# The gates of the last 128 tokens: scattered into DRAM by adding transfers instead of built by matmuls

## The reference, cut to what matters

```
idx  = i1[ci // 16] * 128 + i2[ci % 16]                 # 16 experts of each head and token
gate = softmax(sc)                                      # over the 16
act  = gelu(einsum('thed,td->the', u_table[idx], x))    # u, v: 16384 x 1024
y    = einsum('the,thed->td', gate * act, v_table[idx])
```

## Time and profile before

| | |
|---|---|
| median of 3 runs | 1456.25 us (1448.58 to 1458.06) |
| profiled execution | 1457.33 us, its span 1455.5 us |
| granted TensorE clock, mean | 0.995 |
| busy: PE, DVE, POOL, ACT | 98%, 82%, 53%, 44% |
| moved by DMA | 423.15 MB, 291 GB/s over the span |

### The profile page before, as it was taken

How to read it: one execution, slowest core, us unless ns; L and a number is a source line. 1 busy time by engine, 2 the same in 40 slices (tenths; PEclk the granted TensorE clock), 3 DMA queues, 4 the chain that set the end, 5 groups by cost and what they waited for, 6 DMA issues and landing times.

```text
span 1455.5 us, 24698 instructions
## 1 busy us (share of the span) xinstructions
PE 1427.1 (98%) x8813; PEld 1367.2 (94%) x8813; DVE 1187.4 (82%) x2337; ACT 637.1 (44%) x1035; POOL 768.0 (53%) x428
## 2 busy tenths in 40 slices
PE   7999889999999999999999999899999999999998
PEld 6879678888999999999999999899999999999998
DVE  5747463388989999989999897678899998998994
ACT  4463472222433333447777775332343333433332
POOL 2524171233577678865555555256566665566630
PEclk9999999999999999999999999999999999999999
DMA  7400211322579989999999999989999999999991
GB/s 271 152 30 1 116 30 47 106 69 72 165 249 351 319 311 346 411 391 333 365 363 350 363 395 393 396 304 410 410 410 410 410 409 410 411 410 410 410 360 58
DMA packets 165902, 423.15 MB, mean 291 GB/s; under 512 B 13348, under 2 KB 85924, under 8 KB 163912
## 3 DMA queue, kind: packets, MB, share of 16 engines
q1 hardware_dynamic: 119624, 254.48, 46.9%
q0 software_dynamic: 46208, 167.81, 30.2%
HBM read 376.00 MB, written 46.20 MB: 290 GB/s over the span
## 4 chain that ended last, share of the span: by engine, by line
PE 91%; DMA 4%; DVE 2%; issue 1%; ACT 1%; DVEq 0%; SPq 0%; ACTq 0%
PE banks L2052 33%; PE banks L1816 16%; PE banks L2123 10%; PE banks L2125 10%; PE banks L2124 10%; PE banks L2091 5%; DMA act_in<-act_scratch 3%; PE banks L2031 1%; PE banks L1846 1%; DMA u_raw<-in_uT 1%; PE banks L1890 1%; PE banks L1948 1%; PE banks L1968 1%; PE banks L1967 1%; DVE x_res L1635 1%
## 5 line engine op out<-in xcount | busy, mean ns | idle before, releaser
L822 POOL DMA_INDIRECT rows<-in_v,idx x160 | 286.1, 1788 | 189.2 <-DVE x_res L1635 129.0
L2123 PE MATMUL banks<-w_hi,v_hi 128*128 128x352 f32 x1024 | 330.0, 322 | 1.8 <-DVE w_lo L1734 1.7
L2124 PE MATMUL banks<-w_lo,v_hi 128*128 128x352 f32 x1024 | 329.3, 322 | 0.0
L2125 PE MATMUL banks<-w_hi,v_lo 128*128 128x352 f32 x1024 | 329.3, 322 | 0.0
L1161 ACT ACTIVATE v_hi<-v_raw 128x1024 fp32r<-128x1024 f32 x128 | 134.5, 1059 | 287.3 <-DMA v_raw<-in_v 287.0
L822 POOL DMA_INDIRECT rows<-in_u,idx x160 | 191.1, 1195 | 122.0 <-DVE z L1617 85.5
L798 POOL TENSOR_TENSOR u_lo<-u_raw,u_hi 128x1024 fp32r<-128x1024 f32 x66 | 164.0, 2488 | 95.4 <-ACT u_hi L1056 52.7
L2052 PE MATMUL banks<-h_lo,u_hi 128*128 128x352 f32 x1024 | 198.0, 328 | 0.0
L2123 PEld LDWEIGHTS banks<-w_hi,v_hi 128*128 128x128 f32 x1024 | 192.3, 188 | 2.8 <-issue 2.6
L2052 PE MATMUL banks<-h_hi,u_hi 128*128 128x352 f32 x1024 | 191.2, 328 | 3.7 <-ACT act_kept L1082 3.7
L2124 PEld LDWEIGHTS banks<-w_lo,v_hi 128*128 128x128 f32 x1024 | 192.3, 188 | 0.0
(11 more groups left out here) (284 smaller groups left out, 2084.7 us busy)
## 6 DMA issues: line engine op xcount, KB each, us to landing
u_raw<-in_uT SPq DMA_DIRECT2D x128, 512.0 KB, 6.7
v_raw<-in_v SPq DMA_DIRECT2D x128, 512.0 KB, 15.5
gate_scratch<-stage SPq DMA_DIRECT2D x11, 2048.0 KB, 12.1
gate_pairs<-gate_scratch SPq DMA_DIRECT2D x15, 1408.0 KB, 18.3
act_scratch<-act_out SPq DMA_DIRECT2D x116, 176.0 KB, 7.0
act_in<-act_scratch SPq DMA_DIRECT2D x29, 704.0 KB, 16.0
wi_raw<-in_w_in SPq DMA_DIRECT2D x8, 1024.0 KB, 7.2
wq_raw<-in_w_q SPq DMA_DIRECT2D x8, 1024.0 KB, 5.6
```

The costliest lines, as they stand in the source:

```text
L822: nc.gpsimd.indirect_dma_start(ROW_KB[U_SLOT[s]][:], None, a["u"] if kind in "ab" else v_flat, bass.IndirectOffsetOnAxis(ap=at_x, axis=0)) ...
L2123: mm(y, v_hi[x][:, ds], w_hi[q][:, j, :], start=start, stop=False)
L2124: mm(y, v_hi[x][:, ds], w_lo[q][:, j, :], start=False, stop=False)
L2125: return mm(y, v_lo[x][:, ds], w_hi[q][:, j, :], start=False, stop=stop)
```

## The change

- The dense tokens 384 to 511 get no gate matrices. `BUILT` chunks (7 of 11) are built: 224 tokens, 56 batches. Blocks before the gates are 88 (`PRE`), the blocks with gates 88 to 119.
- Their part of the gates' DRAM tensor is cleared by 16 transfers of 512 KB on SP's queue in the first part, from a tile of zeros.
- GpSimd scatters their gates: for each of the 128 slots one indirect transfer with addition, 128 elements of 4 bytes from column `x` of `tri` to cells whose numbers are in `idx3`. Three or four scatters follow each block from 66 to 112, 16 in five blocks and none in the sixth; before the first of a head GpSimd waits until all scatters of the head before have landed, since two heads may add to one cell.
- `choose(3)` computes the cell numbers in floats on VectorE instead of row and column tiles.
- Low parts of u: up to block 63 GpSimd makes three of four (before: one of two), then one of four.
- Dots: 1.25 for each block up to 61, then about 1.7.

```
-PRE_BODY, PRE_TRIPS = 4, 18
-MAIN_BODY, MAIN_TRIPS = 8, 6
+BUILT = CHUNKS - P // CHUNK
+BATCHES = BUILT * CHUNK // BATCH
+PRE_BODY, PRE_TRIPS = 4, 22
+MAIN_BODY, MAIN_TRIPS = 8, 4
...
+SHARED = [n for n in range(SHARE_FROM, POST) if (n % 4 != 3 if n < TRI_TRIP * PRE_BODY else n % 4 == 0)]
+SCATTER = {66 + 6 * h + j: (h, (0, 4, 7, 10, 13, 16)[j:j + 2]) for h in range(PH) for j in range(5)}
+DOTS = [""] * POST + ["aa"] * 3 + ["a"] + [""] * 4
+for _n in range(SHARE_FROM - 2, POST):
+    DOTS[_n] = "a" * (1 + (_n % 4 == 3 if _n < NORM_AT else _n % 2 or _n % 8 == 2 or _n % 16 == 6))
+for _n in range(NORM_AT, PRE + 2 * MAIN_BODY):
+    if "".join(DOTS).count("b") < NE:
+        DOTS[_n] = DOTS[_n][:-1] + "b"
...
+            def clear(m):
+                sp.dma_start(gate_d[m, :, BUILT:].rearrange("p c n t -> p (c n t)").rearrange("p (x e) -> p x e", e=P),
+                             zeros[:].unsqueeze(1).to_broadcast([P, (CHUNKS - BUILT) * PAIR * CHUNK // P, P])).then_inc(gates_cleared, 16)
+            sp.wait_ge(zeros_ready, 1)
             for r in range(3, UNITS):
                 load_unit(r)
+                for m in range(2):
+                    clear(2 * (r - 3) + m)
...
+            def scatter(h, k0, k1):
+                if h == k0 == 0:
+                    pool.wait_ge(idx3_ready, 1)
+                    pool.wait_ge(tri_ready, 2 * (TB - 2) + 1)
+                    pool.wait_ge(gates_cleared, 16 * NK // PAIR)
+                if k0 == 0 and h:
+                    pool.wait_ge(gates_scattered, 16 * TOPK * h)
+                for x in range(h * TOPK + k0, h * TOPK + k1):
+                    nc.gpsimd.indirect_dma_start(
+                        gate_cells, bass.IndirectOffsetOnAxis(ap=idx3[:, x:x + 1], axis=0),
+                        tri[:, TB - 2, 0, x:x + 1], None, compute_op=ALU.add).then_inc(gates_scattered, 16)
...
                     pool.wait_ge(share_open, SHARED.index(n + 2) + 1)
                     split_u(n + 2)
+                if n in SCATTER:
+                    h, (k0, k1) = SCATTER[n]
+                    scatter(h, k0, k1)
...
+            sp.wait_ge(gates_scattered, 16 * SLOTS)
             sp.dma_start(gates[:].rearrange("p c n t -> p c (n t)"), half_pair(SAVED // PAIR, 1)).then_inc(gates_in, 16)
```

More of the change, by code:

```diff
@@ L66 @@
 V_ATT, V_ML, V_CQ, V_CKV, V_BI, V_BF = 0, 8, 12, 14, 15, 16
-V_W = 17
+V_AT = 17
+V_W = 18
 E_BLOCKS = NK
@@ L100 @@
 assert MAIN_BATCHES * MAIN_TRIPS >= BATCHES > MAIN_BATCHES * (MAIN_TRIPS - 1) and MAIN_BATCHES * BATCH == 2 * CHUNK
-EXP_TRIP, TRI_TRIP = PRE_TRIPS - 3, PRE_TRIPS - 2
+EXP_TRIP, TRI_TRIP = 15, 16
 NORM_AT, TAB_AT = 62, 68
[L105 to L113, removed]
+SHARED = [n for n in range(SHARE_FROM, POST) if (n % 4 != 3 if n < TRI_TRIP * PRE_BODY else n % 4 == 0)]
[6 more added lines that the diff above has]
+        DOTS[_n] = DOTS[_n][:-1] + "b"
 U_DOTS = SLOTS + NE
@@ L119 @@
 assert ALL_DOTS.count("b") == NE
-assert ALL_DOTS.count("a") == SLOTS
+assert ALL_DOTS.count("a") == SLOTS, ALL_DOTS.count("a")
 ALL_DOTS += "w" * (NE - ALL_DOTS.count("w")) + "v" * SLOTS
@@ L129 @@
 DOTS_PRE = dots_before(PRE)
-GELU_TRIP = 4
+GELU_TRIP = 2
 ADDS_LEFT = GATHERS - dots_before(E_BLOCKS)
@@ L335, in build @@
         acc_b = at("acc_b", 182, [P, D])
+        zeros = at("zeros", 207.25, [P, P])
+        idx3 = at("idx3", 204, [P, SLOTS], I32)
         idx0 = at("idx0", 20, [P, SLOTS], I32)
@@ L436, in build @@
         tri_ready = sem("tri_ready")
+        zeros_ready = sem("zeros_ready")
+        gates_cleared = sem("gates_cleared")
+        gates_scattered = sem("gates_scattered")
+        idx3_ready = sem("idx3_ready")
         triT_done = sem("triT_done")
@@ L500, in lo_slot, with low_parts, wait_ulo @@
             return n % 4 if n < POST else n % 2
-        def wait_ulo(eng, i, base, body):
+        def low_parts(n):
+            at_pool = min(n + 1, POOL_FIRST) + sum(m <= n for m in SHARED)
+            return (ulo_pool, at_pool) if n < POOL_FIRST or n in SHARED else (ulo_dve, n + 1 - at_pool)
+        def wait_ulo(eng, i, base, body, trip=1):
             if isinstance(i, int):
[L505 to L517, removed]
+                eng.wait_ge(*low_parts(i * body + base))
+                return
+            made, at_trip = low_parts(trip * body + base)
+            each = low_parts((trip + 1) * body + base)[1] - at_trip
+            eng.wait_ge(made, i * each + (at_trip - trip * each))
         def staged_at(b):
@@ L553, in _ @@
             sp.dma_start(pos_i[:], a["positions"]).then_inc(pos_in, 16)
+            def clear(m):
+                sp.dma_start(gate_d[m, :, BUILT:].rearrange("p c n t -> p (c n t)").rearrange("p (x e) -> p x e", e=P),
+                             zeros[:].unsqueeze(1).to_broadcast([P, (CHUNKS - BUILT) * PAIR * CHUNK // P, P])).then_inc(gates_cleared, 16)
+            sp.wait_ge(zeros_ready, 1)
             for r in range(3, UNITS):
                 load_unit(r)
+                for m in range(2):
+                    clear(2 * (r - 3) + m)
             arrived(sp, ("S", H - 1, TB - 1))
             sp.dma_start(w_out[:], a["w_out"].rearrange("(k p) n -> p k n", p=P)).then_inc(wout_in, 16)
+            for m in range(2 * (UNITS - 3), NK // PAIR):
+                clear(m)
             arrived(sp, ("pv", *attention_units()[-1]))
@@ L594, in save_act, with pre @@
                              act_out[:, j % RING, :]).then_inc(act_saved[j % RING], 16)
-            def pre(i):
+            def pre(i, trip=1):
                 for j in range(PRE_BODY):
                     n = i * PRE_BODY + j
-                    wait_ulo(sp, i, j, PRE_BODY)
+                    wait_ulo(sp, i, j, PRE_BODY, trip)
                     load_u(n + 4, j)
@@ L611, in _ @@
                         sp.dma_start(h2x[x * NE:(x + 1) * NE, :], h2x_d).then_inc(h2x_in, 16)
-            with sp.Fori(SHARE_FROM // PRE_BODY, PRE_TRIPS) as i:
-                pre(i)
+            with sp.Fori(SHARE_FROM // PRE_BODY, TRI_TRIP) as i:
+                pre(i, SHARE_FROM // PRE_BODY)
+            with sp.Fori(TRI_TRIP, PRE_TRIPS) as i:
+                pre(i, TRI_TRIP)
             def save_gates(i, chunk):
@@ L631, in main @@
                         save_gates(i - 1, 1)
-            sp.wait_ge(tri_ready, 2 * (TB - 1) + 1)
+            sp.wait_ge(tri_ready, 2 * (TB - 2) + 1)
             for y in range(P // NE):
@@ L671, in _ @@
                 sp.wait_ge(act_saved[q], 16 * SAVED // RING)
-            sp.wait_ge(gate_saved[1], 16 * (CHUNKS // 2))
-            sp.wait_ge(gate_saved[0], 16 * (CHUNKS + 1) // 2)
+            sp.wait_ge(gate_saved[1], 16 * (BUILT // 2))
+            sp.wait_ge(gate_saved[0], 16 * ((BUILT + 1) // 2))
+            sp.wait_ge(gates_scattered, 16 * SLOTS)
             sp.dma_start(gates[:].rearrange("p c n t -> p c (n t)"), half_pair(SAVED // PAIR, 1)).then_inc(gates_in, 16)
@@ L734, in _ @@
             nc.gpsimd.memset(ones_sq[:], 1.0).then_inc(rr_ready, 1)
+            nc.gpsimd.memset(zeros[:], 0.0).then_inc(zeros_ready, 1)
             def scale_heads(rows, last):
@@ L815, in gather_u @@
                 if s == U_DOTS:
-                    pool.wait_ge(gate_saved[1], 16 * (CHUNKS // 2))
+                    pool.wait_ge(gate_saved[1], 16 * (BUILT // 2))
                 if s == U_LATE:
@@ L1586, in choose @@
                 settle()
+                if t == TB - 1:
+                    cell, two = pay_f[:, 0, :, :], pay_f[:, 1, :, :]
+                    step(nc.vector.tensor_copy(cell, e_i[:, 1, :, :]))
+                    step(nc.vector.tensor_copy(two, e_i[:, 2, :, :]))
+                    step(nc.vector.tensor_scalar(e_i[:, 0, :, :], e_i[:, 0, :, :], 10, None, ALU.logical_shift_right))
+                    settle()
+                    step(nc.vector.tensor_scalar(cell, cell, float(CHUNK), None, ALU.mult))
+                    step(nc.vector.tensor_scalar(two, two, float(CHUNKS * PAIR * CHUNK), None, ALU.mult))
+                    step(nc.vector.tensor_copy(sc_f[:], e_i[:, 0, :, :]))
+                    yield
+                    settle()
+                    step(nc.vector.tensor_tensor(cell, cell, two, ALU.add))
+                    step(nc.vector.tensor_scalar(sc_f[:], sc_f[:], float(P * CHUNKS * PAIR * CHUNK - PAIR * CHUNK), None,
+                                                 ALU.mult))
+                    settle()
+                    step(nc.vector.tensor_tensor(cell, cell, sc_f[:], ALU.add))
+                    settle()
+                    step(nc.vector.tensor_scalar(cell, cell, vecs[:, V_AT:V_AT + 1], None, ALU.add))
+                    yield
+                    settle()
+                    nc.vector.tensor_copy(idx3[:].rearrange("p (h k) -> p h k", h=PH), cell).then_inc(idx3_ready, 1)
+                    return
                 for s in range(2):
@@ L1671, in _ @@
                 if n == TAB_AT:
-                    for t in range(TB - 1):
+                    for t in range(TB - 2):
```

(16 more changed lines are left out.)

4 lines of the change are left out of this document (2 added, 2 removed).

## The result

The changed kernel took 1601.55 us (1597.87 to 1605.35, 4 runs), the one before 1453.13 beside it: 1.1025 times as long, 95% interval 1.0978 to 1.1072. The prediction was 1491 us with a range to 1545: slower was right, by how much was not. The profiled execution took 1604.5 us, its span 1602.5.

A forecast was written before the change was run, and what follows sets the result against it. The prediction took GpSimd, given the scatters, to become the bound: TensorE waits 73.1 - 7.7 = 65.4 us, less 31.7 saved, is +33.7 on the profiled 1457.3, so 1491 us. Range 1432 to 1545.

The forecast's parts named there:

- What is saved, -31.7 us: TensorE's path: 32 gate batches fewer 28.2 us, gates beginning 16 blocks later 3.2, three transposes fewer 0.3.
- The term for the first stretch, 11.2 late: Iterations 18 to 61: GpSimd's 178.4 us of work against TensorE's 167.2, so GpSimd 11.2 us late.
- counted 0 for VectorE: VectorE's dropped row operands and changed casts were given 0; a few us if VectorE became late.
- The clearing, 0: Sixteen 512 KB writes on SP's queue while DMA engines stand nearly idle: taken as 0, at most +3 us.
- The nearest row is the gather: GpSimd's scatter, absent from the trace, was priced like a gather: 1.32 us pitch, taken between 1.245 and 1.39.
- the upper bound of 1.98: Upper bound for a scatter's GpSimd time: median gather of v, 1.68 us, and 0.30; the lower was 0.52.
- the same ledger: GpSimd's work against TensorE's by stretch: 11.2, 51.1 and 10.8 us late, less 7.7 of cover for low parts, less 31.7.
- How it is handed on: GpSimd's lateness reaches TensorE through low parts it still makes, queued behind scatters: 65.4 us of waiting.
- Waits between heads, 0: GpSimd's 7 waits for the last head's scatters to land: taken as 0, +25 us at the median landing time.
- the signs named: If right: scatters 1.25 to 1.4 us apart, GpSimd over 95% busy blocks 62 to 113, TensorE waits 5 to 10 us.
- A dear scatter: Rival: scatter takes 1.98 us of GpSimd, +118, 1576 us; chance 0.12 together with DMA engines as the bound.
- The DMA engines as the bound: Rival: scatter packets at 0.152 us each fill the DMA engines, +134, 1591 us; chance 0.12 together with dear scatter.

The follow-up runs named there:

- no_scatter: Changed kernel without its 128 scatters and SP's wait for them, cells still cleared: 1429.97 us, ratio 0.986 to the kernel before.
- even_deal: Changed kernel with u's low parts before block 64 dealt as before, every second block to GpSimd: 1609.71 us, ratio 1.106 to the kernel before.
- half_slots: Changed kernel with only the 64 even-numbered slots scattered, with addition: 1490.51 us, ratio 1.024 to the kernel before.
- lo_off_pool: Changed kernel with all low parts of u from block 64 on made by VectorE, none by GpSimd: 1573.0 us, ratio 1.084 to the kernel before.
- pack_32: Whole-result version scattering only the last 32 tokens, four slots side by side, 32 adding scatters instead of 128: 1468.71 us, ratio 1.014 to the kernel before.

## Why the prediction was right or wrong

1. **What is saved, -31.7 us: right.** no_scatter ran at 1429.97 where 1457.3 - 31.7 + 3.5 = 1429 was expected. 448 gate matmuls are left. Part of the match is luck: blocks 17 to 61 took 6.1 us more than their sum and 113 to 127 3.0 more than before, 87 to 113 took 4.1 less than 149.8, and block 17 began 4.2 us earlier than in the trace of before. The term for the first stretch, 11.2 late, is luck too: TensorE took 10.7 us more there (177.9 against 167.2), but even_deal, with less work for GpSimd and a longer stretch, shows that it was not GpSimd's time. The prediction had counted 0 for VectorE, because it had "no wait on the path"; in the kernel before it was busy 208.84 of 220 us from 420 us on the earlier trace rows.
2. **The clearing, 0: right**, as far as the times up to block 17 show.
3. **The step that failed: "The nearest row is the gather ... I take ... 1.32 us, for both kinds."** A scatter with addition took 2.06, above even the upper bound of 1.98. Two terms are in it: the addition costs 0.6 us (1.553 against 0.965 at least), and the stretching, for which I had put 0.07 us above the undisturbed pitch, is 0.2: the means stand that much above the minimum for adding and writing scatters. By the timelines the 54 adding scatters with a `TENSOR_TENSOR` of VectorE beside them last 1.92 us in the mean, the 74 others 1.64. With 2.06 and 1.41 the same ledger gives blocks 62 to 87 17.9 + 55.0 + 125.7 - 98.8 = 99.8, blocks 88 to 113 15.4 + 60.6 + 138.0 - 149.8 = 64.2, the sum 11.2 + 99.8 + 64.2 - 7.7 - 31.7 = +135.8: 1593 us, against 1604.5 of the profiled execution. The mechanism held from block 61 on: GpSimd set the pace. 128 x 0.74 us of one mis-sized price were 95 of the 113 us by which I was off. Only the sum is met, not its parts: over the 98.8 and 149.8 us of TensorE's own work the two stretches took 76.3 and 81.3 us more, since 11 of the 61 scatters counted in the first were still to come when TensorE reached block 87.
4. **The rest, about 10 us:** blocks 113 to 127 took 76.3 instead of 65.1. The ledger ends at 113, but GpSimd's lateness is handed on behind it. half_slots shows besides that a stretch can lose 18.8 us with GpSimd's sum at or under TensorE's.
5. **How it is handed on: half right.** Low parts on GpSimd are one channel (78.8 us); gate rows on VectorE, behind dots behind gathers, are another (60.4) that the prediction did not price. lo_off_pool shows that closing the first gives back hardly more than the low parts' own time: what counts is GpSimd's total, as long as GpSimd is full.
6. **Waits between heads, 0: nearly right**, 2.6 us. Of the signs named, the 448 gate matmuls came; GpSimd's busy share from 640 to 1030 us was 84% (327.5 of 390) and not over 95, because the pauses of 0.30 us are not counted as busy; TensorE waited eight times for GpSimd's low parts, 9.9 us in the mean but up to 20.7.
7. **The rivals.** "A dear scatter" (1576 us, within a chance of 0.12) is what happened, beyond its own bound. The DMA engines as the bound are refuted: their share fell, and time follows GpSimd's pitch and not the packets. The range ended at 1545 because I gave little to an addition that the trace had never shown; the upper bound should have been the range's end.

## What to carry to other kernels

An indirect transfer cost the issuing engine one instruction's time whatever its bytes (at least 0.93 us for 128 rows of 4 KB, 0.97 for 128 numbers of 4 bytes): weigh it as time of that engine (here 2.06 us each with addition, against 0.22 us of TensorE for a token's gates), and first ask how much of that engine is free. When a price has no row, and the operation does more than its nearest relative, let the range reach past the upper row. And the lateness of a full engine found its way to TensorE through whatever waited behind it: with the low parts moved away, the wait moved to gate rows and VectorE's low parts.

## What the runs showed of the hardware that I had not expected

- An indirect transfer of 128 elements lasts at least 0.965 us on GpSimd when it writes, 1.553 when it adds; with 64 elements and addition 1.397.
- Of the 12 scatters of the changed kernel directly behind a low part of GpSimd, eight last 2.40 to 2.75 us and four 1.62 to 2.01, where the median of all is 1.595. The low part alone does not explain it: in pack_32 six of eight last 1.61 or 1.62. Each of the eight long ones has beside it either VectorE's low part or a dot of VectorE that lasts 1.34 to 2.69 us instead of 1.21. What holds up what is not separated.
- TensorE ran slowly at first after a long wait. In the changed kernel, after 17.90 us without work, groups of 8 matmuls:

```profile
677.88 2.71 PE L2110 MATMUL banks<-h_hi,u_lo 128*128 128x352 f32 x8 [17.90 <-POOL u_lo L815]
680.39 2.34 PE L2110 MATMUL banks<-h_hi,u_hi 128*128 128x352 f32 x8
682.58 1.49 PE L2110 MATMUL banks<-h_lo,u_hi 128*128 128x352 f32 x8
```

The second starts 2.51 us after the first, 0.31 a matmul, beside 0.158 in the kernel before. The granted clock had fallen while TensorE did nothing: 1.00 of full speed from 660 to 664 us, 0.50 from 668 to 677, still 0.50 from 677.9 to 680.3 (the level of 1.2 GHz), and 1.00 again, 2.4 GHz, from 682.6 on. GpSimd set the pace of that stretch, so the slow matmuls are no term of the sum; no run separates what they cost.
